# Two 64-row half tiles side by side in the expert stage, and expert rows added in DRAM by scatters

## The reference

```python
s = jax.nn.sigmoid((x @ w_router).astype(jnp.float32))
...                                                     # best group of 4, best 2 experts in it
gate = gate / jnp.sum(gate, -1, keepdims=True)
combine = jnp.sum(jax.nn.one_hot(eidx, N_EXPERTS, dtype=jnp.float32) * gate[..., None], axis=1)
hg = jnp.einsum('nd,edf->nef', x, wg)                   # 1024 -> 256, for each expert
hu = jnp.einsum('nd,edf->nef', x, wu)
act = jax.nn.silu(hg) * hu * combine[:, :, None].astype(x.dtype)
y = jnp.einsum('nef,efd->nd', act, wd)                  # 256 -> 1024, summed over the experts
...
h = layer_norm(ALPHA * h + f, P['ln3_g'][l], P['ln3_b'][l])
```

## Time and profile before

| | |
|---|---|
| median of 3 runs | 1721.78 us (1715.70, 1721.78, 1722.27) |
| the profiled execution | 1715.85 us, of which 1714.0 us from the first to the last instruction |
| granted clock of TensorE, mean | 0.924 of 2.4 GHz |
| busy: PE, DVE, ACT, POOL | 1475.0, 649.9, 499.7, 170.2 us |

### The profile page before, as it was taken

One profiled execution on the slowest core, in us unless ns is written; L12 is line 12 of the kernel. 1 busy time (PEld: TensorE's weight loads), 2 busy tenths in 40 slices (PEclk: granted clock), 3 DMA queues, 4 the chain that ended last, 5 costly groups with the idle time before them and its releaser, 6 DMA issues. The chain is left out here.

```text
span 1714.0 us, 24653 instructions
## 1 busy us (share of the span) xinstructions
PE 1475.0 (86%) x9685; PEld 1055.9 (62%) x9686; DVE 649.9 (38%) x1019; ACT 499.7 (29%) x1050; POOL 170.2 (10%) x162
## 2 busy tenths in 40 slices
PE   4998999689999898889979899898369999999910
PEld 2445999545597677768879877686144455444400
DVE  4223362377512234457631033565511111111158
ACT  1114133277605334441122244322001111111122
POOL 0000000024200232200000000000020000000046
PEclk9998999789979799999989999999669999999965
DMA  8110111160013400031041263400739775522153
GB/s 308 55 56 20 54 43 37 36 191 8 1 49 101 136 15 3 3 101 68 38 138 35 84 260 128 154 1 11 311 123 337 294 302 218 197 98 86 62 209 143
DMA packets 85871, 193.36 MB, mean 113 GB/s; under 512 B 13092, under 2 KB 49067, under 8 KB 79363
## 3 DMA queue, kind: packets, MB, share of 16 engines
q1 hardware_dynamic: 74011, 148.49, 24.6%
q0 software_dynamic: 7008, 25.43, 4.2%
q10 hardware_dynamic: 4752, 18.02, 2.6%
HBM read 152.83 MB, written 39.18 MB: 112 GB/s over the span
## 5 line engine op out<-in xcount | busy, mean ns | idle before, releaser
L2977 PE MATMUL bank<-arena,hT 128*128 x512 | 232.3, 597 | 2.2 <-DVE hT L3084 2.2
L2977 PEld LDWEIGHTS bank<-arena,hT 128*128 128x128 f32 x512 | 95.8, 192 | 110.6 <-issue 110.6
L2997 PE MATMUL bank<-arena,hT 128*128 x256 | 115.3, 593 | 1.6 <-ACT hT L3035 1.6
L472 PE MATMUL bank<-arena,hT 128*128 128x512 f32 x256 | 111.8, 595 | 0.0
L3080 DVE TENSOR_TENSOR hT<-bank,hT 128x256 f32<-128x256 f32 x32 | 13.6, 424 | 216.4 <-ACT hT L3041 216.4
L2133 PE MATMUL bank<-hT_rest,f_w_high 128*128 128x352 f32 x288 | 93.8, 326 | 0.0
L2947 POOL DMA_INDIRECT hT<-tokens,row_token x32 | 34.1, 1067 | 587.8 <-PE bank L2963 307.0
L472 PEld LDWEIGHTS bank<-arena,hT 128*128 128x128 f32 x256 | 48.4, 192 | 57.7 <-issue 57.6
L2997 PEld LDWEIGHTS bank<-arena,hT 128*128 128x128 f32 x256 | 46.4, 191 | 48.1 <-issue 48.1
L2132 PE MATMUL bank<-hT_high,q_w_high 128*128 128x352 f32 x192 | 62.5, 326 | 4.0 <-DVE q_w_low L2421 4.0
L2132 PE MATMUL bank<-f_h_high_a,f_w_high 128*128 128x352 f32 x180 | 59.3, 329 | 6.7 <-DVE f_w_low L682 6.7
(11 more groups left out here) (465 smaller groups left out, 2978.2 us busy)
## 6 DMA issues: line engine op xcount, KB each, us to landing
arena<-in_ex_wg_dram SPq DMA_DIRECT2D x16, 1024.0 KB, 6.2
arena<-in_ex_wu_dram SPq DMA_DIRECT2D x16, 1024.0 KB, 8.8
arena<-in_ex_wd_dram SPq DMA_DIRECT2D x16, 1024.0 KB, 10.8
expert_rows<-hT ACTq DMA_DIRECT2D x32, 512.0 KB, 2.7
tokens<-h SPq DMA_DIRECT2D x16, 512.0 KB, 2.8
arena<-in_cache_mem_k_dram SPq DMA_DIRECT2D x8, 1024.0 KB, 4.9
arena<-in_w_in_dram SPq DMA_DIRECT2D x12, 512.0 KB, 3.9
h<-tokens SPq DMA_DIRECT2D x6, 1024.0 KB, 7.0
```

Source lines behind the costliest of these rows:

```text
L472: last = nc.tensor.matmul(ps[bank][0:r, 0:n], hT[:, k, i * P:i * P + r], wt[:, k, col:col + n], start=(k == 0), stop=(k == KC - 1))
L2977: last = nc.tensor.matmul(ps[UPB[u % 2]][:, :], xT[:, u % 2, k, :], gate_up_of[:, bass.ds(slot, 1), :, k, :].rearrange("p a g f -> p (a g) ...
L2997: last = nc.tensor.matmul(ps[DNB[q]][:, :], hidT[:, u % 2, f, :], down_of[:, bass.ds(slot, 1), f, q * 512:(q + 1) * 512].rearrange("p a n ...
```

## The change

Experts get half tiles of 64 rows instead of tiles of 128. There are 48 half tiles, the most that could be needed, and two of them, of the same or of two experts, share one tile of 128 rows: 24 tiles instead of 32. In the products of PE the lower half tile uses columns 0 to 63 of the array and the upper one columns 64 to 127, each with its own weights, so that there are two products of 64 x 512 where there was one of 128 x 512. The lower half reads its weights from the slot of its expert. The weights of the upper half are first copied (`copy_weights`) to one of two buffers, one in the arena and one in the place of `h`, which the stage no longer needs: ACT and DVE copy 3 x 1024 floats per partition each, per tile. The gate is now applied to the hidden rows (`row_gate`).

The rows of `h` are no longer kept in SBUF: the stage before stores them twice in DRAM, as `tokens` to gather from and as `expert_sums` to add to. POOL adds the two halves of `y` to `expert_sums` with two scatters per tile (64 rows each, the second after the first has landed). `stage_combine` loads the sums and does the layer norm, with `h` divided by ALPHA throughout.

```diff
-MOE_TILES = (2 * TOK - NE) // P + NE
+HT_ROWS = 64
+HALVES = (2 * TOK - NE) // HT_ROWS + NE
+MOE_TILES = (HALVES + 1) // 2
...
 # stage_residual, SP
+                for p, i in enumerate(order):
+                    sp.wait_ge(normed, p + 1)
+                    for dst in (c.tokens_dram, c.sums_dram):
+                        sp.dma_start(dst[i * P:i * P + rows(i), :], h[0:rows(i), i, :]).then_inc(c.h_out, 16)
...
 # stage_route, PE
+            for n in range(2 * TILES):
+                last = nc.tensor.matmul(ps[5][:, 0:MOE_TILES], one_lo[:, n, :], one_gate[:, n, :],
+                                        start=(n == 0), stop=(n == 2 * TILES - 1))
+            last.then_inc(rows_ok, 1)
+            pe.wait_ge(slots_ok, 1)
+            nc.tensor.matmul(ps[6][0:HT_ROWS, 0:MOE_TILES], K("ident")[:, HT_ROWS:P], c.A("slot_f"), start=True, stop=True).then_inc(rows_ok, 1)
...
 # stage_experts
+    copies = [c.A("wb"), h.rearrange("p i d -> p (i d)")[:, 0:3 * EW]]
+    def copy_weights(eng, copy, t, u, z):
+        e = eng.value_load(c.tile_expert[0:1, bass.ds(2 * t + 1, 1)], min_val=0, max_val=NE - 1)
+        eng.wait_ge(w_ok, e + 1)
+        copy(whole[u % 2][:, :, z, :], slots[:, bass.ds(e & 3, 1), :, z, :].rearrange("p a q n -> p (a q) n")).then_inc(wb_ok[z], 1)
...
 # POOL
+            def add_rows(t):
+                gp.wait_ge(y_ok[0], t + 1)
+                gp.wait_ge(y_ok[1], t + 2)
+                for half in range(2):
+                    q = slice(half * HT_ROWS, (half + 1) * HT_ROWS)
+                    if t + half >= 1:
+                        gp.wait_ge(y_out, 16 * (2 * t + half))
+                    gp.indirect_dma_start(c.sums_dram, bass.IndirectOffsetOnAxis(ap=row_slot[half][0:HT_ROWS, t:t + 1], axis=0),
+                                          y[q, t % 2, :], None, compute_op=ALU.add).then_inc(y_out, 16)
...
+            for t in range(MOE_TILES):
+                if t + 2 < MOE_TILES:
+                    gather(t + 2)
+                if t >= 1:
+                    add_rows(t - 1)
+            add_rows(MOE_TILES - 1)
+            gp.wait_ge(y_out, 32 * MOE_TILES)
...
 # PE, gate_up (product_down alike)
+                if half == 0:
+                    for q in range(2):
+                        pe.wait_ge(wb_ok[q], t + 1)
-                    last = nc.tensor.matmul(ps[UPB[u % 2]][:, :], xT[:, u % 2, k, :], gate_up_of[:, bass.ds(slot, 1), :, k, :].rearrange("p a g f -> p (a g) f"), start=(k == 0), stop=(k == KC - 1))
+                    nc.tensor.matmul(ps[UPB[u % 2]][rows_of(0), :], xT[:, u % 2, k, rows_of(0)],
+                                     gate_up_of[:, bass.ds(slot, 1), :, k, :].rearrange("p a g f -> p (a g) f"),
+                                     start=(k == 0), stop=(k == KC - 1))
+                    last = nc.tensor.matmul(ps[UPB[u % 2]][rows_of(1), :], xT[:, u % 2, k, rows_of(1)], gate_up_b[u % 2][:, :, k, :],
+                                            start=(k == 0), stop=(k == KC - 1))
...
 # ACT, end of finish and of a step (DVE alike, its finish waits for all of the down product)
-                act.wait_ge(y_ok[0], t + 1)
-                act.wait_ge(y_ok[1], t + 2)
-                act.dma_start(c.rows_dram[bass.ds(t, 1)].rearrange("a p d -> (a p) d"), y[:, u % 2, :]).then_inc(y_out[u % 2], 16)
+                if not (last and u == U - 1):
+                    if not (first and u == 0):
+                        act.wait_ge(down, 2 * t)
+                    copy_weights(act, nc.scalar.copy, t + 1, u + 1, 0)
...
 # stage_combine, SP; gather and the two additions per tile are gone
+            for i in range(TILES):
+                sp.dma_start(h[0:rows(i), i, :], c.sums_dram[i * P:i * P + rows(i), :]).then_inc(h_in[i], 16)
```

More of the change, by code:

```diff
@@ L104 @@
 NCONST = len(CONSTS) * P
+MAXH = (TOK + HT_ROWS - 1) // HT_ROWS
 def route_blocks():
@@ L2918, in stage_experts @@
     x_in = [s(f"x{u}") for u in range(2)]
-    y_out = [s(f"y{u}") for u in range(2)]
+    y_out = s("y")
     xT_ok = [s(f"xT{q}") for q in range(2)]
     y_ok = [s(f"yok{q}") for q in range(2)]
-    x_turned, up, sig, hid_ok, hid_turned, hidT_ok, down, scaled = (
-        s("xturned"), s("up"), s("sig"), s("hid"), s("hturned"), s("hidT"), s("down"), s("scaled"))
+    x_turned, up, sig, hid_ok, hid_turned, hidT_ok, down = (
+        s("xturned"), s("up"), s("sig"), s("hid"), s("hturned"), s("hidT"), s("down"))
     U = 4
     J = MOE_TILES // U
+    wb_ok = [s(f"wb{q}") for q in range(2)]
+    c.place(start=4 * 3 * EW, wb=3 * EW)
+    copies = [c.A("wb"), h.rearrange("p i d -> p (i d)")[:, 0:3 * EW]]
+    gate_up_b = [x[:, 0:2 * EW].rearrange("p (g k f) -> p g k f", g=2, k=KC) for x in copies]
+    down_b = [x[:, 2 * EW:].rearrange("p (j n) -> p j n", j=2) for x in copies]
+    whole = [x.rearrange("p (q z n) -> p q z n", q=3, z=2) for x in copies]
+    slots = c.xw.rearrange("p s (q z n) -> p s q z n", q=3, z=2)
+    def copy_weights(eng, copy, t, u, z):
+        e = eng.value_load(c.tile_expert[0:1, bass.ds(2 * t + 1, 1)], min_val=0, max_val=NE - 1)
+        eng.wait_ge(w_ok, e + 1)
+        copy(whole[u % 2][:, :, z, :], slots[:, bass.ds(e & 3, 1), :, z, :].rearrange("p a q n -> p (a q) n")).then_inc(wb_ok[z], 1)
     XT, UPB, HT, DNB = (0, 1), (2, 3), 4, (6, 7)
@@ L3003, in step @@
                 prev = (j, u - 1) if u else (j - 1, U - 1)
-                e = expert(j * U + u)
-                prev_e = None if first else expert(j * U + u - 1)
+                e = expert(2 * (j * U + u))
+                prev_e = None if first else expert(2 * (j * U + u - 1))
                 gate_up(j, u, 0, e)
@@ L3096, in step @@
                 if not (first and u == 0):
-                    finish(j * U + u - 1, j * 2 + (u - 1) // 2, (u - 1) % U, first and u < 3)
+                    finish(j * U + u - 1, (u - 1) % U, first and u < 3)
+                if not (last and u == U - 1):
+                    copy_weights(dve, nc.vector.tensor_copy, j * U + u + 1, u + 1, 1)
             turned_x(0, 0)
-            nc.vector.tensor_scalar(h[:, 0:NT, :], h[:, 0:NT, :], ALPHA, None, ALU.mult).then_inc(scaled, 1)
-            nc.vector.tensor_scalar(h[0:NS, NT, :], h[0:NS, NT, :], ALPHA, None, ALU.mult).then_inc(scaled, 1)
+            copy_weights(dve, nc.vector.tensor_copy, 0, 0, 1)
             for u in range(U):
@@ L3162, in _, with moments @@
             link = Chain(dve, dve_chain)
[L3164 to L3173 removed]
+            nc.vector.memset(c.eps3, LN_EPS / ALPHA ** 2).then_inc(eps_ok, 1)
+            def moments(i):
+                dve.wait_ge(h_in[i], 16)
                 if i >= 2:
@@ L3183, in _ @@
             for i in range(TILES):
-                sum_up(i)
+                moments(i)
                 if i == 0:
```

172 lines of the change are left out of this document (85 added, 87 removed).

## The result

The changed kernel takes 1788.62 us (median of four runs, 1786.42 to 1795.55), the kernel before 1718.74 (four runs): a ratio of 1.0416, 95% interval 1.0392 to 1.0441, slower. The forecast was 1770, with a range of 1728 to 1825. The profiled execution of after is the longest of the four, 1795.55 us with a span of 1793.8; against the span of before, 1714.0, that is +79.8.

| Stretch | before | after | difference | forecast |
|---|---|---|---|---|
| start to the route stage | 1197.1 | 1202.7 | +5.6 | 0 |
| route stage to the first transposes of the experts | 64.8 | 74.0 | +9.2 | +9 |
| from there to the last copy of `y` | 373.2 | 448.1 | +75.0 | +65.7 |
| from there to the first load of the combine stage | 3.9 | 23.6 | +19.7 | +12 |
| combine stage | 75.0 | 45.3 | -29.7 | -32.5 |

A forecast was written before the change was run, and what follows sets the result against it. It took a never-idle PE to bound the expert stage, DVE and POOL the combine stage. Terms 18.2 + 47.5 + 12 + 9 - 32.5 = +54.2 on 1715.85 gave 1770 us; range 1728 to 1815, extended to 1825 for rivals.

The forecast's parts named there:

- Slower, by the pause and the clock: Expert stage: copy waits and a lowered PE clock make the kernel slower; chance of slower 0.87.
- the pause: Between tiles on PE: the whole weight copy is a gap, 4.1 us, set by ACT; loop +18.2 before the clock.
- the clock term: PE in the expert stage: nine gaps in ten lower the clock, 2.2 us lost each, +47.5 in all.
- Pairs: PE's column halves: two products run at once, 0.43 per pair, what one product cost.
- The two rivals on them: PE's column halves: weight loads don't hide, 1846 us, chance 0.04; halves run one after the other, 2017 us, chance 0.02.
- Turning the array's form: PE between transposes and column halves: four turns a tile at 0.09 us, 0.36 a tile.
- The 0.1 for the upper half's later start: PE, each tile: the second half starts behind the first, some 0.1 us.
- The scatter tail: End of expert stage: four bare scatters need 20.2 us; combine starts 15.2 after the last `y`, where it was 3.2: +12.
- 0.4 for the stage's end: Between the last scatter's landing and the combine stage: closing the expert stage takes 0.4 us.
- Scatters in the loop at no cost: POOL's queue in the expert loop: 11.0 us a tile, under the tile's 18, so no cost.
- Route: Route stage: second one-hot product, 36 more records at half clock, 7.89 us, plus 1 for longer tables: +9.
- Combine: Combine stage: first gain ends after 9.3 us, then 3.55 per tile; 42.5 instead of 75.0: -32.5.

The follow-up runs named there:

- two parts: Changed kernel with the same weight copies split: gate and up copied earlier, down after its down product, a semaphore each; 1668.77 us, ratio 0.972 to the kernel before.
- the pause filled: Changed kernel with constant products into an unused bank behind each down product; with four products 1737.92 us, ratio 1.014 to the kernel before.
- the eight-product run: Changed kernel with eight constant products of 128 x 512 into an unused bank behind each down product; 1806.44 us, ratio 1.051 to the kernel before.
- the run without the upper scatters: Kernel with copies in two parts, scatters of the upper halves left out, so another output; 1628.80 us, ratio 0.950 to the kernel before.
- the merged kernel: Kernel with copies in two parts, combine stage inside the expert stage's block, last wait on SP, gain and shift loaded earlier; 1662.59 us, ratio 0.969.
- the run without copies: Changed kernel without all weight copies but the first two, so another output; 1673.67 us, ratio 0.974 to the kernel before.

## Why the prediction was right, and where its sizes were off

- *Slower, by the pause and the clock:* right, and shown. Without the wait the same copies are free (two parts), and with the pause filled the clock term alone goes. All four errors of size below point the same way: 9.3 in the loop, 7.7 at its end, 2.8 in the combine stage and 0.2 in the route stage are the 20.0 between 54.2 and 74.2.
- *Pairs:* 0.43, as forecast; weight loads hide. The two rivals on them fell.
- *The pause:* 4.09 for 4.1, and ACT decides. Inside it two parts were off and cancelled, which is luck: ACT begins 0.89 behind PE's end (1.12 forecast), PE 0.45 behind ACT's (0.25). DVE's copy took 2.29, not 1.8, and with its late start came within 0.18 of being the bound.
- *Turning the array's form:* mis-sized. 0.09 a turn came from one row that leads from four transposes into column groups; here a turn out and back costs 0.35, 0.71 a tile, and with the last pair's length the work is 12.29, not 11.87, as the eight-product run shows. The 0.1 for the upper half's later start was 0.01; the 0.16 of the last pair stood in no term.
- *The clock:* mis-sized by a little. 1.98 per tile was forecast (nine pauses in ten, 4.5 us of low work); it is 2.36, with 6.05 and 3.40 us of low work in turn and no tile spared in the 19 of the window. Of all 23 pauses one was spared, not one in ten.
- *Both together* make a tile 18.70 in place of 17.95. The first step has no down product and no hidden rows to transpose (14.77 us), and the pause behind it is the one that left the clock at full (16.36 for the next step), so that 23 tiles took 423.7 us (first products at 1282.58 and 1706.24), 10.8 over the forecast; the two ends of the stage gave 1.5 back: the table's +9.3.
- *The scatter tail:* the sum of four landings was right (20.5 for 20.2; issue 1.41, landing 3.6, for 1.05 and 4.0). The step that failed is "0.4 for the stage's end": it was read where POOL had closed the stage long before. POOL's closing instruction of 5.9 us stood in the trace of before and was not looked for; the rest of the 7.7 is some 0.7 from the copy of `y` to the first issue, 0.8 because the last two `y` were 4.7 apart and not 5.5, and the 0.3 of the landings.
- *Scatters in the loop at no cost:* right for an 18.7 us tile, PE's waits name the copies alone. It is the next bound, from a landing of 4.2 us in a 12.13 us tile.
- *Route:* 9.2 for 9. *Combine:* -29.7 for -32.5; the first gain was mis-sized by 3.2, as the loads of gain and shift ahead of the second tile were left out.
- *Readings:* the rows at 1401.88 and 1413.29 are the first half of gate and up, not the second; the 11.41 between them stands. The bounds of the range add up to 1725 and 1820, not 1728 and 1815; the range as given holds the result either way.
- The remaining 5.6 us of the profiled difference lies ahead of the change: with the same code up to there, the twelve other executions reach the route stage up to 2.2 us earlier and 7.2 us later than the kernel before.

## What to carry to other kernels

A copy that waits for the buffer which the product directly ahead has read is bare in full (4.09 us a tile here), and it costs a second time where the pause lowers the clock (2.36 us more); give each part of the buffer its own semaphore, released by its own last reader, before asking for a faster copy. When an engine's last work moves to the end of a stage, look for what that engine does when it closes the stage: its price is in the old trace, hidden. And when the bound goes, work out at which size the next queue binds in the shorter period.

## What the runs showed of the hardware that was not expected

- POOL's closing instruction behind indirect DMAs took 5.88 and 5.93 us, and 6.05 behind the last issue where it was begun early. Its length is not fixed, since it took 3.97 in the run without the upper scatters, and what sets it stays open. It can be overlapped with the landing, and in the merged kernel it moved to the program's end.
- A scatter of 64 rows that adds in DRAM takes POOL 1.41 to issue, 2.14 beside the copies of the weights on DVE and ACT (1.43 at the same place in the run without copies), and lands 3.6 us behind its issue, but 7 to 9 beside an expert's load of 3 MB.
- The clock falls behind pauses of 2.80 us too, in most tiles, where one of 2.40 had left it at full and one of 3.67 in the changed kernel did too: the length of the pause alone doesn't decide.
